# Latent-attention logits as three one-pass products, with four raw weight buffers

## The reference

```python
for layer in range(DEPTH):
    h = rms_norm(x, attn_norm_g[layer])
    c_q, c_kv, k_rope, dq, dk, dv = jnp.split(h @ w_in[layer], splits, axis=-1)
    # latent attention
    q = (rms_norm(c_q, q_norm_g) @ w_uq).reshape(b, s, 8, 128 + 64)
    kv = (rms_norm(c_kv, kv_norm_g) @ w_ukv).reshape(b, s, 8, 128 + 128)
    q_nope = rms_norm(q[..., :128], qn_nope_g);  k_nope = rms_norm(kv[..., :128], kn_nope_g)
    q_rope = apply_rope(rms_norm(q[..., 128:], qn_rope_g), pos);  v = kv[..., 128:]
    sc = (jnp.einsum('bqhn,bkhn->bhqk', qn, k_nope) + jnp.einsum('bqhr,bkr->bhqk', qr, k_r))
    p = jax.nn.softmax(sc * scale, axis=-1);  o_a = jnp.einsum('bhqk,bkhv->bqhv', p, v)
    # ... differential attention o_b ...
    merged = g_a * (o_a @ w_branch_a[layer]) + g_b * (o_b @ w_branch_b[layer])
    x = x + merged @ w_out[layer]
    # feed-forward: dense SwiGLU in layer 0, top-2-of-8 expert SwiGLU in layer 1
```

## Time and profile before

| | us |
|---|---|
| median of 3 runs | 1735.83 |
| lowest, highest | 1735.57, 1738.25 |
| the profiled execution | 1735.91 |
| its span | 1734.1 |
| PE busy | 1719.9 (99%) |
| DVE busy, ACT busy | 1384.5 (80%), 1173.3 (68%) |

### The profile page before, as it was taken

One profiled execution on the slowest core, in us unless ns is written; L12 is line 12 of the kernel. 1 busy time (PEld: TensorE's weight loads), 2 busy tenths in 40 slices (PEclk: granted clock), 3 DMA queues, 4 the chain that ended last, 5 costly groups with the idle time before them and its releaser, 6 DMA issues.

```text
span 1734.1 us, 23591 instructions
## 1 busy us (share of the span) xinstructions
PE 1719.9 (99%) x8188; PEld 1421.3 (82%) x8188; DVE 1384.5 (80%) x1357; ACT 1173.3 (68%) x1241; POOL 68.4 (4%) x93
## 2 busy tenths in 40 slices
PE   9999999999999999999999999999999999999998
PEld 8788888888887878887888888888888888888886
DVE  6876876545477678769988898888888888988996
ACT  7665765444366666657777777777777777777774
POOL 1300000000012000010000000000000000000000
PEclk9999999999999999999999999999999999999999
DMA  7434355555464334669999999999999999999991
GB/s 296 167 122 146 115 175 172 194 186 180 153 216 165 127 101 143 232 285 403 382 364 392 384 369 371 379 386 370 375 398 371 371 377 391 374 375 373 396 391 52
DMA packets 70456, 486.32 MB, mean 280 GB/s; under 512 B 8048, under 2 KB 8816, under 8 KB 13296
## 3 DMA queue, kind: packets, MB, share of 16 engines
q1 hardware_dynamic: 67760, 475.94, 72.9%
q0 software_dynamic: 2624, 9.44, 1.5%
HBM read 479.58 MB, written 5.77 MB: 280 GB/s over the span
## 4 chain that ended last, share of the span: by engine, by line
PE 91%; DVE 4%; DMA 1%; DVEq 1%; issue 1%; ACT 1%; POOL 1%; SPq 0%; POOLq 0%; ACTq 0%
PE ps_proj L1071 12%; PE ps_proj L1075 11%; PE ps_proj L1074 11%; PE ps_proj L599 7%; PE ps_proj L602 7%; PE ps_proj L601 7%; PE ps_score L1071 6%; PE ps_score L1074 6%; PE ps_score L1075 6%; PE ps_trans L630 2%; PE ps_score L593 2%; PE ps_ctx L593 2%; PE ps_score L602 2%; PE ps_score L599 2%; PE ps_score L601 2%; DVE raw_r L1786 2%
## 5 line engine op out<-in xcount | busy, mean ns | idle before, releaser
L2428 DVE TENSOR_TENSOR w_raw_r<-w_raw,hi 128x2048 fp32r<-128x2048 f32 x333 | 751.4, 2290 | 101.5 <-ACT hi L1667 86.5
L1667 ACT ACTIVATE hi<-w_raw 128x2048 fp32r<-128x2048 f32 x332 | 632.2, 1918 | 166.4 <-PE ps_score L1071 62.4
L1071 PE MATMUL ps_proj<-hi,he_hi 128*128 128x512 f32 x896 | 355.7, 397 | 0.0
L1075 PE MATMUL ps_proj<-w_raw_r,he_hi 128*128 128x512 f32 x896 | 349.9, 391 | 0.0
L1074 PE MATMUL ps_proj<-hi,he_lo 128*128 128x512 f32 x896 | 348.8, 389 | 0.0
L1786 DVE TENSOR_TENSOR raw_r<-raw,hi 128x2048 fp32r<-128x2048 f32 (+1 forms) x114 | 257.9, 2272 | 36.4 <-ACT hi L1242 29.9
L1242 ACT ACTIVATE hi<-raw 128x2048 fp32r<-128x2048 f32 (+1 forms) x114 | 215.7, 1895 | 91.3 <-PE ps_proj L601 42.4
L1075 PEld LDWEIGHTS ps_proj<-w_raw_r,he_hi 128*128 128x128 f32 x896 | 168.2, 188 | 36.3
L599 PE MATMUL ps_proj<-hi,hT_hi 128*128 128x512 f32 (+2 forms) x496 | 196.6, 396 | 0.4 <-DVEq L1772 0.4
L1071 PEld LDWEIGHTS ps_proj<-hi,he_hi 128*128 128x128 f32 x896 | 168.3, 188 | 34.0 <-issue 1.5
L1074 PEld LDWEIGHTS ps_proj<-hi,he_lo 128*128 128x128 f32 x896 | 168.5, 188 | 33.1
(11 more groups left out here) (418 smaller groups left out, 1998.2 us busy)
## 6 DMA issues: line engine op xcount, KB each, us to landing
w_raw<-in_w_exp SPq DMA_DIRECT2D x336, 1024.0 KB, 7.0
raw<-in_w_pre SPq DMA_DIRECT2D x110, 1024.0 KB, 4.9
y_rows<-y_sent POOLq DMA_DIRECT2D x7, 512.0 KB, 9.0
raw<-in_w_pre SPq DMA_DIRECT2D x4, 640.0 KB, 6.4
raw<-in_w_pre SPq DMA_DIRECT2D x2, 512.0 KB, 5.5
h_rows<-htok SPq DMA_DIRECT2D x1, 1024.0 KB, 5.0
out_rows<-x_tok SPq DMA_DIRECT2D x4, 256.0 KB, 3.1
x_tok<-in_x_rows SPq DMA_DIRECT2D x2, 256.0 KB, 4.4
```

The costliest lines, as they stand in the source:

```text
L1071: m = nc.tensor.matmul(o, a_hi, w_h, start=first, stop=False)
L1075: return nc.tensor.matmul(o, a_hi, w_l, start=False, stop=last)
L1667: A(w_hi[k % HS][:], w_raw[n], ACT.Copy).then_inc(gran_hi, 1)
L2428: V.tensor_tensor(w_low[k % WS], w_raw[k % WS], w_hi[k % HS][:].bitcast(F32), ALU.subtract)\
```

## The change

The high part of the latent queries and keys is now written by ACT as fp32r (`turned_nope`), and DVE writes the low part (`low_nope`), gain times PSUM minus high, into two new tensors. The low tensors take the room of two raw buffers: RAW is 4. PE makes three one-pass matmuls for each of the former float32 ones. The `trans` bank of these turns is now given back by DVE, after its low part, and no longer by ACT. The first pair of a group of heads waits for the low parts (`nope_ready`). The expert buffers are ordered anew, so that the two that lie on the low tensors are among the first six.

```diff
-RAW, HIGH = 6, 4
+RAW, HIGH = 4, 4
+        qnT_lo, knT_lo = (keep(n, [HEADS, T], F32R) for n in ("qnT_lo", "knT_lo"))
-            freed = [at + 32] * 4 + [at + 36, at + 37, at + 38] + [at + 40] * 4 + [at + 39, at + 40, at + 41]
+            freed = [at + 32] * 6 + [at + 38, at + 39] + [at + 40] * 4 + [at + 40, at + 41]
...
+                    pe.wait_ge(nope_ready, nth(NOPE, l, "kn0b" if i == 0 else "qn1b"))
                     for v, o, _ in pair:
                         for q in range(TT):
-                            mm(o[:, q * T:(q + 1) * T], qnT[:, v, q * P:(q + 1) * P], knT[:, v], q, 4)
+                            cols, rows = slice(q * T, (q + 1) * T), slice(q * P, (q + 1) * P)
+                            mm(o[:, cols], qnT_hi[:, v, rows], knT_hi[:, v], q, 4)
+                            mm(o[:, cols], qnT_lo[:, v, rows], knT_hi[:, v], 1, 4)
+                            mm(o[:, cols], qnT_hi[:, v, rows], knT_lo[:, v], 1, 4)
...
+            def turned_nope(l, z, tensor, gain, first=0):
+                for j, half in enumerate("ab"):
+                    o = of(l, z + half)
+                    A(two(tensor, (first + 2 * j) // 2), o[:], ACT.Identity, scale=g_(l, gain)).then_inc(operand, 1)
...
-                turned_op(l, "kn0", knT, "kn")
+                turned_nope(l, "kn0", knT_hi, "kn")
...
+            def low_nope(l, z, hi_, lo_, gain, first=0):
+                for j, half in enumerate("ab"):
+                    o = of(l, z + half)
+                    dve.wait_ge(operand, nth(OPERANDS, l, z + half))
+                    n = (first + 2 * j) // 2
+                    V.scalar_tensor_tensor(two(lo_, n), o[:], g_(l, gain), two(hi_, n).bitcast(F32), ALU.mult,
+                                           ALU.subtract).then_inc(nope_ready, 1)
+                    gave(l, z + half)
...
                 scale(l, "kn1")
+                low_nope(l, "kn0", knT_hi, knT_lo, "kn")
                 lo(at + 15)
```

More of the change, by code:

```diff
@@ L88 @@
 CHUNKS = ("kv", "cq", "dq0", "dk0", "qr", "qn0", "kn0", "kn1", "qn1", "dq1", "dk1")
+NOPE = ("qn0a", "qn0b", "kn0a", "kn0b", "kn1a", "kn1b", "qn1a", "qn1b")
 OPERANDS = ("KR", "dq0a", "dq0b", "dk0a", "dk0b", "qn0a", "qn0b", "qra", "qrb", "kn0a", "kn0b", "kn1a", "kn1b",
@@ L276, in build @@
         x_tok = keep("x_tok", [TT, D])
-        raw_at = [top[0] + n * 4 * PIECE for n in range(RAW)]
+        raw_at = [top[0] + n * 4 * PIECE for n in range(RAW + 2)]
         raw = [keep(f"raw{n}", [PIECE]) for n in range(RAW)]
+        qnT_lo, knT_lo = (keep(n, [HEADS, T], F32R) for n in ("qnT_lo", "knT_lo"))
         low = [place(f"raw{n}_r", [PIECE], raw_at[n], F32R) for n in range(RAW)]
@@ L294, in build @@
         merged = place("merged", [TT, D], base + 36 * K)
-        qnT = place("qnT", [HEADS, T], base + 44 * K)
-        knT = place("knT", [HEADS, T], base + 52 * K)
+        qnT_hi = place("qnT_hi", [HEADS, T], base + 44 * K, F32R)
+        knT_hi = place("knT_hi", [HEADS, T], base + 52 * K, F32R)
         gates = place("gates", [TT, 2 * D], base + 44 * K)
@@ L322, in build @@
         hidT = [place(n, [4, T], base + at * K, F32R) for n, at in (("dhT_hi", 24), ("dhT_lo", 28))]
-        w_at = [base + n * 8 * K for n in range(4)] + [raw_at[1], raw_at[2], raw_at[3]] \
-            + [base + (36 + n * 8) * K for n in range(4)] + [raw_at[4], raw_at[5], raw_at[0]]
+        w_at = [base + n * 8 * K for n in range(4)] + [raw_at[4], raw_at[5], raw_at[3], raw_at[0]] \
+            + [base + (36 + n * 8) * K for n in range(4)] + [raw_at[1], raw_at[2]]
         w_raw = [place(f"w_raw{n}", [GRAN], at)[:] for n, at in enumerate(w_at)]
@@ L393, in build @@
         diff_exp = sem("diff_exp")
+        nope_ready = sem("nope_ready")
         diff_prob = sem("diff_prob")
@@ L1458, in attention @@
                 hi(at + 15)
-                turned_op(l, "qn0", qnT, "qn")
+                turned_nope(l, "qn0", qnT_hi, "qn")
                 roots_of(l, "kn0")
@@ L1468, in attention @@
                 exps(0)
-                turned_op(l, "kn1", knT, "kn", 4)
+                turned_nope(l, "kn1", knT_hi, "kn", 4)
                 for u in range(1, 2 * HEADS):
@@ L1497, in attention @@
                     if u == 2:
-                        turned_op(l, "qn1", qnT, "qn", 4)
+                        turned_nope(l, "qn1", qnT_hi, "qn", 4)
                     if u == 4:
@@ L2058, in attention @@
                 group_sums(l, "kn0")
+                low_nope(l, "qn0", qnT_hi, qnT_lo, "qn")
                 scale(l, "kn0")
@@ L2068, in attention @@
                 weights(0)
+                low_nope(l, "kn1", knT_hi, knT_lo, "kn", 4)
                 for u in range(1, 2 * HEADS):
@@ L2085, in attention @@
                     weights(u)
+                    if u == 2:
+                        low_nope(l, "qn1", qnT_hi, qnT_lo, "qn", 4)
                 ob_copy(HEADS - 2)
```

## The result

The changed kernel takes 1795.48 us (median of 5 runs, 1794.41 to 1801.97) against 1736.04: ratio 1.0351, 95% interval 1.0339 to 1.0363. The profiled execution is the longest of the five (span 1800.2 us). It lost 6.3 us in its first 41 us.

A forecast was written before the change was run, and what follows sets the result against it. PE was taken as the bound, busy 1719.9 of 1734.1 us. Waits of 23.6 (A, B, C, both layers), 5.1 (D), 11.5 (E) and 1.0 (F), less 3.0 for products, add 38.2 to 1735.9: 1774.1 us, range 1754 to 1792.

The forecast's parts named there:

- Four raw buffers: Weight loads leave two pieces later and land 4.9 us after release; ACT stands still up to 5 us, copies behind it too.
- A: The v product, once a layer: PE waits for ACT's copy behind a late high part, 4.6 us.
- C: First pair of heads, once a layer: PE waits for the low keys queued on DVE, 4.1 us (bounds 3.1 and 6).
- D: Entry of the dense part, once: a late high part delays the copies ahead of PE's first dense product, 5.1 us.
- E: Dense chunks 1 to 5: PE waits at the second turn of the hidden values, 2.3 us each, 11.5 in all.
- B: Turns of the latent queries (qr), once a layer: PE waits for the second trans bank and qn0's scaling, together 3.1 us.
- F: Entry of layer 1: a late high part on ACT ahead of the norm statistics, 1 us (bounds 0 and 5.1).
- rival 3: PE runs at half speed after five waits of over 4 us, 3 us lost each, 15 in all: 1789 us; chance 0.09.
- The products: One-pass matmuls in the 128-row part of the pairs gain 0.37 us a pair, 3.0 us over eight pairs.
- Rival 1: Slack absorbs the late loads before ACT's copies are due, only the products count: 1733 us; chance 0.05.
- rival 2: Only the fronts of the layers pay, the dense part hides its share: 1757.5 us; chance 0.11.
- rival 4: One-pass products cost 0.23 us each in the pairs, so 7.6 us are lost, not 3.0 won: 1785 us; chance 0.03.

The follow-up runs named there:

- kernel 1: The kernel before with four raw buffers and nothing else, no one-pass products or low parts: 1788.46 us, ratio 1.0306.
- kernel 5: The changed kernel with many of ACT's high parts moved later in its list and the low keys earlier on DVE, still four raw buffers: 1741.83 us, ratio 1.0036.
- Kernel 3: The changed kernel with six raw buffers, its low queries and keys placed in unused parts of other tensors: 1746.11 us, ratio 1.0058.
- kernel 6: The changed kernel with one call moved: piece 12's high part behind the copies of the v product's first half on ACT: 1790.22 us, ratio 1.0310.
- kernel 7: The changed kernel with nine extra one-pass products on PE ahead of the second turn in dense chunks 1 to 4: 1791.56 us, ratio 1.0333.

## Why the prediction was wrong

The sign and the mechanism were right, the size was not: 38.2 forecast, 59.4 measured.

- **Four raw buffers: right.** ACT waited 191.6 us for loads that had left late, and the copies behind it stood still. Kernels 1 and 5 show both halves: the loss comes with the buffers, and goes with the order.
- **The waits at A, C, D and E: right** within 0.4 us each (4.6 and 4.98; 4.1 and 4.27, though 2.90 in layer 1; 5.1 and 5.03; 2.3 and 2.30 to 2.46). B was low: 3.1 against 3.7 and 4.5. F was 1.6 where I took 1. Kernel 3 shows that C is a cost of its own, and not of the buffers.
- **D's second wait: missed.** I followed the first two copies of the hidden state behind piece 43, and not the next two behind piece 44: 2.6 us.
- **The step that failed is the clock.** The sum priced every wait at its length. The third rival, 9 in 100, had the mechanism, but only for waits over 4 us, for five places and 15 us. The clock fell behind waits of 2.30 to 2.46 us as well, in four of the five chunks. 15.3 us of the 21.2 that the forecast lacks are this. Some 3 more are waits longer than forecast, most of it D's second, 0.8 is the products, and some 2 us are in neither. The Trainium skill (TensorE: Matmul & The Clock Gate, section "HAM oscillation — how this bites in real kernels") says that bursts parted by DMA waits can each start at the lower clock; this trace agrees, though PE's waits here name ACT and DVE and not each was followed by it: 0.50 behind 10 of the 12 waits of over 2.2 us (and behind one of 1.98 at the start). I had drawn the line at 4 us from nothing in the trace, since none of its waits was longer than 1.8 us. The bound there should have been open: with rival 3's own 3 us behind each of the 13 forecast waits, 39 us more.
- **The products: right in sign, less in size.** From the first matmul to the rotary part a later pair takes 1.70 us against 1.82, and PE gains 0.27 us a pair, not 0.37: from one pair to the next it takes 17.18 us where it took 17.45. One reason is that the first matmul there is followed only after 0.31 us. Over eight pairs that is 2.2 us and not 3.0. The loop over heads and the experts behaved as forecast: no wait of more than 0.4 us was added there.

Rival 1 (slack absorbs) would need what five buffers give; rival 2 is out, since the dense part with its entry paid 27.5 us; rival 3 was right in its mechanism and too small; rival 4 is out by the 0.12 us between starts.

What stays open: why this profiled execution lost 6.3 us at the start, where load 5 took 7.5 us (kernel 6 lost as much there, kernels 1 and 7 1.0 and 0.2). In both that lost it, PE's first wait for x was the longest, 1.98 and 2.12 us against 1.25 at most, and the clock fell behind it; that this is the cause isn't shown. Open too is what decides whether the clock falls. Its fall isn't a matter of the wait's length alone: behind 2.36 us at 358 it fell, behind 2.38 at 328 and 2.90 at 626 it did not, and at 829 it fell with no wait at all.

## What to carry to other kernels

When a buffer is taken away, don't ask whether the last consumer still gets its data in time; ask which engine takes its list in order in front of the data, and what stands behind that instruction. A wait for a load there is paid by others, unless the release is earlier than the engine's turn by more than the load's flight (here one piece of 5.5 us against 4.9). Move the work that waits for the transfer behind the work that someone waits for: that gave 54 us back with no byte more of memory.

Price a new wait on TensorE as its length and half of the time at the lower clock behind it: here 1.5 to 1.6 us on 2.4, and 1.5 to 2.7 on 4.3 to 5. It is a price to allow for and not a certain one: behind four waits of 2.1 to 2.9 us nothing was lost.

## What was not expected of the hardware

- TensorE, idle for 2.30 to 2.46 us with 1.00 in the rows ahead of it, came back at 1.2 GHz for some 3 us of work (0.50 in the rows), four times in the dense part; nine useless products kept it up.
- A wait of the same length doesn't always do it: in kernel 1 it stayed at 1.00 behind chunk 1's 2.33 us and fell behind chunk 2's 2.33. Five runs of the changed kernel spread over 7.6 us, those of the kernel before over 2.7; how much of that is the clock isn't shown.
